# The routed experts' down weights requested from ScalarE's DMA queue instead of SyncE's

## What is computed

```python
# h: (576, 1024); every token goes to 8 of 64 experts
s = sigmoid(h @ w_router);  eidx = top-8 experts of each token, by groups
for each block (expert e, up to 128 of its tokens tok, their weights wt):
    xb = h[tok]
    hb = silu(xb @ we_g[e]) * (xb @ we_u[e])      # gate and up: 1024 x 256 each
    acc[tok] += wt * (hb @ we_d[e])               # down: 256 x 1024
out = acc + (silu(h @ ws_g) * (h @ ws_u)) @ ws_d  # one shared expert
```

## Time and profile before

| | |
|---|---|
| median of three runs | 1106.46 us |
| the profiled execution's own time | 1108.23 us |
| its span, first to last instruction | 1106.4 us |
| TensorE busy (matmuls) | 1065.5 us, 96% |
| VectorE busy | 729.2 us, 66% |
| ScalarE busy | 215.3 us, 19% |
| SyncE's DMA queue, q1 | 287.32 MB, 64.2% of 16 engines' span |
| GpSimd's DMA queue, q0 | 48.68 MB, 11.6% |
| mean granted TensorE clock | 0.992 |

### The profile page before, as it was taken

How to read it: one execution, slowest core, us unless ns; L and a number is a source line. 1 busy time by engine, 2 the same in 40 slices (tenths; PEclk the granted TensorE clock), 3 DMA queues, 4 the chain that set the end, 5 groups by cost and what they waited for, 6 DMA issues and landing times.

```text
span 1106.4 us, 16559 instructions
## 1 busy us (share of the span) xinstructions
PE 1065.5 (96%) x5954; PEld 535.9 (48%) x5954; DVE 729.2 (66%) x1934; ACT 215.3 (19%) x473; POOL 136.3 (12%) x163
## 2 busy tenths in 40 slices
PE   6999999999999999999999999999899999999797
PEld 3456678777877644664333333333233333333242
DVE  3218441546546645766988888888687987888148
ACT  4131332222233313301111111111011110111111
POOL 0110000000020010111121211111112111121100
PEclk9999999999999999999999999999999999999999
DMA  9958720120352277769999999999999999999798
GB/s 368 339 197 301 244 81 24 53 86 1 115 190 87 77 242 248 293 283 380 409 413 425 424 425 424 422 424 427 422 425 424 423 424 420 412 416 406 255 425 334
DMA packets 51653, 337.11 MB, mean 305 GB/s; under 512 B 9636, under 2 KB 14088, under 8 KB 30830
## 3 DMA queue, kind: packets, MB, share of 16 engines
q1 hardware_dynamic: 33710, 287.32, 64.2%
q0 software_dynamic: 17856, 48.68, 11.6%
HBM read 311.30 MB, written 37.24 MB: 315 GB/s over the span
## 4 chain that ended last, share of the span: by engine, by line
PE 79%; DMA 12%; DVE 5%; ACT 2%; issue 1%; SPq 0%; DVEq 0%; ACTq 0%
PE bank L1594 23%; PE bank L1617 12%; PE bank L1289 10%; DMA mem<-in_w_exp_down 6%; PE bank L1308 5%; PE bank L1407 3%; DMA hT<-in_w_exp_down 3%; PE bank L1408 3%; PE bank L1525 3%; PE bank L1202 3%; PE bank L1286 3%; DMA mem<-in_w_sh_down 2%; PE bank L1703 2%; PE bank L1177 1%; DVE mem L2290 1%
## 5 line engine op out<-in xcount | busy, mean ns | idle before, releaser
L1594 PE MATMUL bank<-mem 128*32 128x512 f32 (+2 forms) x1568 | 334.0, 595 | 1.8 <-DVE mem L2290 1.0
L2290 DVE STREAM_TRANSPOSE mem<-mem 32x256 f32<-32x256 f32 x448 | 195.1, 436 | 5.8
L1617 PE MATMUL bank<-mem 128*32 128x512 f32 (+2 forms) x712 | 178.4, 608 | 10.9 <-DMA mem<-in_w_exp_down 7.0
L1594 PEld LDWEIGHTS bank<-mem 128*32 128x32 f32 (+2 forms) x1568 | 106.9, 128 | 164.9 <-issue 164.9
L1289 PE MATMUL bank<-hT,mem 128*128 128x288 f32 x512 | 133.3, 409 | 1.0 <-ACT mem L968 1.0
L2290 DVE STREAM_TRANSPOSE mem<-x_sb 32x256 f32<-32x256 f32 x240 | 104.5, 435 | 3.1
L1289 PEld LDWEIGHTS bank<-hT,mem 128*128 128x128 f32 x512 | 93.8, 190 | 25.8 <-issue 2.4
L1617 PEld LDWEIGHTS bank<-mem 128*32 128x32 f32 (+2 forms) x712 | 56.8, 133 | 81.4 <-issue 71.1
L1594 PE MATMUL bank<-x_sb,mem 128*32 128x512 f32 (+2 forms) x256 | 87.1, 596 | 0.0
L2306 DVE COPY hT<-bank 128x512 f32<-128x512 f32 x48 | 33.1, 691 | 67.2 <-PE bank L1617 67.1
L822 POOL DMA_INDIRECT mem<-ffn_in_rows,idxg x32 | 32.9, 1030 | 268.0 <-DVE idxs L2274 192.6
(11 more groups left out here) (404 smaller groups left out, 1218.9 us busy)
## 6 DMA issues: line engine op xcount, KB each, us to landing
mem<-k_w_exp SPq DMA_DIRECT2D x54, 2048.0 KB
mem<-in_w_exp_down SPq DMA_DIRECT2D x52, 1024.0 KB
x_sb<-k_w_exp SPq DMA_DIRECT2D x10, 2048.0 KB
mem<-k_w_ada SPq DMA_DIRECT2D x8, 2048.0 KB, 9.2
mem<-k_w_in SPq DMA_DIRECT2D x7, 2048.0 KB, 9.0
hT<-in_w_exp_down SPq DMA_DIRECT2D x12, 1024.0 KB
mem<-expert_out_rows SPq DMA_DIRECT2D x6, 2048.0 KB, 15.7
mem<-k_w_head SPq DMA_DIRECT2D x4, 2048.0 KB, 17.3
```

Source lines behind the costliest of these rows:

```text
L1594: i = mm(bank[sl, :], xT[:, j % 2, c * BLK + sl.start:c * BLK + sl.stop], gu_view(r)[:, c, :], start=c == 0, stop=c == KC - 1)
L1617: i = mm(ps[4 + hf][sl, :], hhT[:, k * BLK + sl.start:k * BLK + sl.stop], dn_view(r)[:, k, hf * 512:(hf + 1) * 512], start=k == 0, stop=k ...
L2290: i = dve.transpose(cols[dl, :, sl], rows[sl, :, dl])
```

## The change

SyncE's list keeps the gate/up loads alone. The 59 down loads that take over another expert's place are asked for by ScalarE, each right behind `out_rows` of the block that frees the place: at most two for one block. Each of them is a register load of the expert's number, a wait on `edn` and a DMA request. ScalarE also waits once for the sorted table (`tab_ready`) before its loop over blocks. The first down loads, lines 661 to 667, stay with SyncE, as does everything after the blocks.

```diff
-            for when, is_dn, r in sorted([(LASTB[q] + 0.5, 0, r) for r, q in enumerate(GU_BEFORE) if q is not None] +
-                                         [(LASTB[q] + 2.0, 1, r) for r, q in enumerate(DN_BEFORE) if q is not None]):
-                if not is_dn:
-                    ids[r] = sp.value_load(ptab[0:1, r:r + 1], min_val=0, max_val=NE - 1)
-                    sp.wait_ge(S["eup"], LASTB[GU_BEFORE[r]] + 1)
-                    load_gate_up(r, ids[r])
-                else:
-                    sp.wait_ge(S["edn"], LASTB[DN_BEFORE[r]] + 1)
-                    load_dn(r, ids.pop(r))
+            for when, r in sorted((LASTB[q], r) for r, q in enumerate(GU_BEFORE) if q is not None):
+                e = sp.value_load(ptab[0:1, r:r + 1], min_val=0, max_val=NE - 1)
+                sp.wait_ge(S["eup"], when + 1)
+                load_gate_up(r, e)
@@ scalar engine @@
+            def next_down(b):
+
+                for r, q in enumerate(DN_BEFORE):
+                    if q is not None and LASTB[q] == b:
+                        e = act.value_load(ptab[0:1, r:r + 1], min_val=0, max_val=NE - 1)
+                        act.wait_ge(S["edn"], b + 1)
+                        act.dma_start(dn_view(r), one_expert("w_exp_down", e).rearrange("(p j) d -> p j d", j=FJ)).then_inc(dn_sem(r), 16)
...
             shared_silu(NSH - 1)
+            act.wait_ge(S["tab_ready"], 1)
             for b in range(NBK):
                 if b >= 1:
                     hhT_evac(b - 1)
@@
                 silu(b, b)
                 if b >= 1:
                     out_rows(b - 1, b - 1)
+                    next_down(b - 1)
```

## The result

| | before | after |
|---|---|---|
| median | 1107.13 us | 1139.11 us |
| ratio, 95% interval | | 1.028 (1.026 to 1.031) |
| the profiled execution | 1108.2 us | 1142.9 us |
| its span | 1106.4 us | 1141.1 us |
| last `down` of the blocks ends | 1042.9 us | 1078.4 us |

The median before is now over four runs, not three. The change makes the kernel 32 us slower. I had forecast no change, and my range ended at 1110.3 us. The profiled executions are 34.7 us apart, and the last `down` ends 35.5 us later, so the whole loss arises inside the block phase. What comes behind it takes 0.8 us of that back.

A forecast was written before the change was run, and what follows sets the result against it. The prediction took the DMA engines to bound the kernel. Its terms, -12.8, +9.6, +3.2 and +0.3 us, took the profiled 1108.2 us to 1108.5, so 1106.8 us against a median of 1106.46; range 1101.5 to 1110.3 us.

The forecast's parts named there:

- The bound: In the block phase the DMA engines set the pace: 11.8 us per block against some 11.1 us for TensorE.
- Step 1: Down loads off SyncE's queue land in 10 us, 18 for a pair's second; TensorE's four waits go, 12.8 us.
- The sum: Removed waits -12.8, gate/up waits +9.6, longer shared-weight wait +3.2, scatter +0.3: 1108.5 us profiled, 1106.8 us expected.
- Step 2: Gate/up loads land 6.9 us later, their 4.2 us left soon goes, and waits at `up` take back 9.6 us.
- Step 3: ScalarE's requests, at most some 2.5 us a block, hide in 4.89 us of idling; otherwise 1 us a block at worst.
- Step 4: SyncE's shorter list gains and loses nothing; three rings of the DMA engines may cost more, or less, than two.
- Step 5: The last block starts and ends 3.2 us earlier (0.1 to 5.1).
- Step 6: After the blocks, shared down weights land unchanged; TensorE waits 7.9 us instead of 4.7; the last scatter adds 0.3 us.
- Rival A: The end isn't pinned to the shared weights' landing: 3.2 us are kept, 1103.3 us, at best 1100.9; chance 0.29.
- Rival B: A third queue costs 0.7% of DMA rate from 520 to 1047 us, 3.7 us: 1110.2 us; chance 0.21.
- Rival C: Queues are served in request order, so TensorE's four waits stay: 1106.5 us plus at most 1 us; chance 0.08.

The follow-up runs named there:

- The inserted work: The kernel before with 12 extra matmuls on TensorE ahead of block 20's first product: 1108.54 us, 1.0015.
- controls: The kernel before, two queues, with smaller pieces: gate/up 8 KB, 1110.79 us; gate/up 8 KB and down 4 KB, 1114.22 us.
- three-queue kernel: The changed kernel with smaller pieces: gate/up 8 KB, 1117.23 us; gate/up 8 KB and down 4 KB, 1120.6 us.

## Why the prediction was wrong, point by point

- **The bound.** Right: the DMA engines set the pace. The inserted work shows it.
- **Step 1, down loads leave SyncE's queue.** Right in what it says of them: all four waits for down weights are gone, and by the 944 completion packets of q10 (16 for each of 59 loads) they land 12.5 us behind their request in the median, where I had 10 and 18. But I priced the load that moves by the gathers' 10.6 us and never priced what the move does to the gathers. **This is the step that failed.** The sum has no term for gathers and scatters that get fewer turns, so it put them at nothing; what the runs showed in its place is TensorE held up by late rows, 27.9 us of idling and 7.6 us of longer matmuls, 35.5 us by the end of the blocks. I had even quoted the rule of turns in its paragraph, and applied it to one of three queues only. GpSimd's queue holds 18.1% of the engines' time and is the one whose transfers are needed within some 10 us.
- **Step 2, gate/up loads overtaken.** Wrong for the changed kernel, whose `up` has no wait that the profile gives to a weight load; its eleven longer waits all end with a turn of rows. Right for the kernel with 8 KB gate/up pieces, where the rows are on time: five waits, 13.8 us. My premise was that the bytes a second stay the same, and they fell from 421 to 394 GB/s.
- **Step 3, ScalarE's work.** Right, hidden: twice as many requests cost at most 0.3%, and their place made little difference.
- **Step 4, three rings.** I left it to bounds of a few microseconds, taken from rates of full queues. Such rows can't price it, for what a third queue takes is not rate but turns from the other two.
- **Step 5, the last block 3.2 us earlier.** It starts at 1062.32 us instead of 1026.63.

```profile
1062.32 5.36 PE L1599 MATMUL bank<-mem 128*32 128x512 f32 x48
...
1074.73 3.64 PE L1622 MATMUL bank<-mem 128*32 128x512 f32 x32 [0.88 <-ACT mem L1093]
1080.55 14.12 PE L1708 MATMUL bank<-mem 128*64 128x512 f32 x32 [2.17 <-issue]
```

- **Step 6, the end pinned by the last byte.** It fell. The wait at line 1708 is 2.17 us instead of 4.71, and no longer for the shared weights, which land at 1076.7 us; the end of the blocks decides. Its premise was wrong for the kernel before too. With the shared weights asked for first they land 8.7 us earlier and nothing is gained: the end follows the landing of the last scatter, and a new order of the same bytes does move single landings. The kernel with 8 KB gate/up pieces shows that it would have fallen even without the starved rows: behind the landing of the last gate/up load stand 16 us of the last block (1035.67 to 1051.7), behind that of the shared weights none of it. If a down load that is not urgent overtakes that gate/up load, the same bytes end the blocks later.
- **Rival A** held that the order of the bytes matters at the end. The kernel with 8 KB gate/up pieces bears that out, but against the change: overtaking made the end later. In the kernel before, with the shared weights asked for first, the order moved their landing and not the end. **Rival B** was right in its sign, and wrong in mechanism and size: at a share of 1.01 to 1.02 three queues move 417 GB/s against 419 and 416 of their controls, so hardly any rate is lost. The share itself fell. **Rival C** had it that the separate queue does nothing; the removed waits refute it.
- **The size.** The sum had -12.8 us of removed waits, to be given back later. In their place stand 27.9 us more of idling and 7.6 us of slower matmuls.

The last 6.4 us of each three-queue kernel over its control lie ahead of the last `down`'s end: for one in longer matmuls and waits at `up` for gate/up loads, for the other in waits for down weights. That the overtaking causes all of this was not tested by itself.

## What to carry to other kernels

Before a class of transfers gets a queue of its own, ask who shares the turns of the DMA engines, not only what the moved class gains. Work out the round (one piece of every full queue, by the duration of each) and set 16 engines / round against the number of small pieces that the kernel needs in a microsecond. In these runs it was the small pieces needed soon, gathers and scatters, that lost to a further queue of large ones. And where the DMA engines set the pace, waits for weights on the compute engine are mostly not time that can be won.

## What the runs showed of the hardware

- Full queues get nearly equal numbers of pieces, whatever their sizes: 238, 245 and 210 in 16 us, 3573, 4011 and 3616 in 127 stretches of 2 us. A queue's share of the bytes thus follows the size of its pieces.
- Smaller pieces at the same bytes cost something of their own: 8 KB instead of 16 KB for gate and up 0.34% (0.23 to 0.46), with 4 KB for down as well 0.62% (0.45 to 0.78).
- Which engine asks was worth next to nothing: all weights from ScalarE's queue took 0.2% longer than all from SyncE's.
- TensorE's branch over an unused part of the program took 4.4 to 7.0 us in the kernels before and after and in the one with the shared weights first. In the last it, and not the weights, held TensorE for 3.8 us behind its last `down`.
